# Fetched rows spread differently over the groups of the values' stage, with VectorE's loop written out

## The reference, cut to what matters

```python
def chunk(args):
    xb, ib, gb = args
    a = jnp.einsum('cd,ced->ce', xb, utab[ib]).astype(jnp.float32)
    coef = (gb * jax.nn.gelu(a, approximate=False)).astype(xb.dtype)
    return jnp.einsum('ce,ced->cd', coef, vtab[ib])
...
x = layer_norm(DN_ALPHA * x + (1.0 + g2) * f, ln2_g[l], ln2_b[l])
```

## Time and profile before

| | |
|---|---|
| median of 3 runs | 3972.95 us (3972.67 to 3986.3) |
| the profiled execution | 3967.34 us, its span 3965.5 us |
| TensorE matmuls | 3678.5 us busy, 93% of the span |
| VectorE | 2550.3 us, 64% |
| ScalarE, GpSimd | 1291.0 and 1165.5 us |
| values' stage | from about 2834 us to the end |

### The profile page before, as it was taken

One profiled execution on the slowest core, in us unless ns is written; L12 is line 12 of the kernel. 1 busy time (PEld: TensorE's weight loads), 2 busy tenths in 40 slices (PEclk: granted clock), 3 DMA queues, 4 the chain that ended last, 5 costly groups with the idle time before them and its releaser, 6 DMA issues. The chain is left out here.

```text
span 3965.5 us, 53964 instructions
## 1 busy us (share of the span) xinstructions
PE 3678.5 (93%) x19170; PEld 3215.8 (81%) x19170; DVE 2550.3 (64%) x5738; ACT 1291.0 (33%) x2513; POOL 1165.5 (29%) x797
## 2 busy tenths in 40 slices
PE   5989899998988889899998999999789999999997
PEld 3679788886766778899998999999668888888875
DVE  5663133221664521578998888988677777777777
ACT  1110122221115221222236787878512222222220
POOL 1133121211333021234443333333253333333340
PEclk9899999998998999999999999999899999999998
DMA  5841212213744222345556999999988888877782
GB/s 191 317 147 40 85 60 76 77 71 140 244 164 176 75 90 74 130 165 200 200 187 207 310 321 308 328 313 322 302 298 291 290 290 289 289 287 286 287 310 112
DMA packets 502716, 827.71 MB, mean 209 GB/s; under 512 B 289047, under 2 KB 309783, under 8 KB 496312
## 3 DMA queue, kind: packets, MB, share of 16 engines
q1 hardware_dynamic: 111848, 371.07, 26.8%
q0 software_dynamic: 84096, 318.80, 22.3%
q10 hardware_dynamic: 306576, 135.28, 13.7%
HBM read 680.35 MB, written 144.70 MB: 208 GB/s over the span
## 5 line engine op out<-in xcount | busy, mean ns | idle before, releaser
L79 PE MATMUL va_fps<-va_vt_h,va_c_h 128*128 128x512 f32 x1536 | 605.2, 394 | 62.4 <-DVE va_vt_l L2286 24.4
L80 PE MATMUL va_fps<-va_vt_l,va_c_h 128*128 128x512 f32 x1536 | 603.4, 393 | 0.0
L81 PE MATMUL va_fps<-va_vt_h,va_c_l 128*128 128x512 f32 x1536 | 602.8, 392 | 0.0
L2164 POOL DMA_INDIRECT va_rows<-in_vtab,k_pick x256 | 398.9, 1558 | 644.3 <-DVE k_big L2310 566.1
L79 PE MATMUL ga_aps<-k_u_h,k_ut_h 128*128 128x384 f32 x1152 | 399.1, 346 | 6.0 <-DVE k_ut_l L2066 4.7
L79 PEld LDWEIGHTS va_fps<-va_vt_h,va_c_h 128*128 128x128 f32 x1536 | 292.1, 190 | 127.6 <-issue 32.8
L1990 ACT ACTIVATE ga_first<-ga_first,ga_gs 128x128 f16<-128x128 f16 x1152 | 357.7, 390 | 105.6 <-DVE ga_first L2049 104.4
L81 PE MATMUL ga_aps<-k_u_h,k_ut_l 128*128 128x384 f32 x1152 | 386.9, 336 | 0.0
L80 PE MATMUL ga_aps<-k_u_l,k_ut_h 128*128 128x384 f32 x1152 | 386.4, 335 | 0.0
L2310 DVE SCALAR_TENSOR_TENSOR k_big<-va_rows,va_coef,k_big 128x1024 f32<-128x1024 f32 x254 | 320.5, 1281 | 59.7 <-DMA va_rows<-in_vtab,k_pick 59.2
L81 PEld LDWEIGHTS va_fps<-va_vt_h,va_c_l 128*128 128x128 f32 x1536 | 291.7, 190 | 61.4
(11 more groups left out here) (305 smaller groups left out, 7949.9 us busy)
## 6 DMA issues: line engine op xcount, KB each, us to landing
k_ut<-in_utab SPq DMA_DIRECT2D x129, 512.0 KB, 5.4
va_vt<-in_vtab SPq DMA_DIRECT2D x128, 512.0 KB, 6.7
va_c<-scratch_ahead SPq DMA_DIRECT2D x128, 384.0 KB, 3.3
va_wt<-scratch_gates SPq DMA_DIRECT2D x128, 384.0 KB, 5.0
hy_tab<-in_tab POOLq DMA_DIRECT2D x64, 512.0 KB, 5.4
scratch_ahead<-ga_gelu_a ACTq DMA_DIRECT2D x72, 384.0 KB, 5.8
sp_wada<-in_w_ada SPq DMA_DIRECT2D x24, 1024.0 KB, 9.1
scratch_gates<-ga_wide ACTq DMA_DIRECT2D x32, 768.0 KB, 13.2
```

Source lines behind the costliest of these rows:

```text
L79: nc.tensor.matmul(out, w[0], x[0], start=first, stop=False)
L80: nc.tensor.matmul(out, w[0], x[1], start=False, stop=False)
L81: return nc.tensor.matmul(out, w[1], x[0], start=False, stop=last)
L2164: nc.gpsimd.indirect_dma_start(got[:, q % SLOTS_G, :], None, vrows, picked(K, q)).then_inc(got_in[q % SLOTS_G], 16)
```

## The change

The number of rows taken in group 0 becomes 4, in group 1 it becomes 8, in groups 2 to 27 it becomes 9, in group 28 it becomes 6 and in group 29 it becomes 4 (again 256 in all). The five places of a group get their rows by an even cut: with nine rows 1, 2, 2, 2 and 2; with eight 1, 2, 1, 2 and 2; with six 1, 1, 1, 1 and 2; with four 0, 1, 1, 1 and 1. The loop over the 26 groups is replaced by straight code, in which the slots' numbers and the waits' values are constants. The sequences of the other four engines are not changed.

```diff
--- before.py
+++ after.py
@@ -2297,26 +2297,26 @@
                 dve.wait_ge(f_mm, j + 1)
                 v.tensor_copy(sums[:, GATHERED + STAY + j, :], wide_banks(STAY)).then_inc(f_ok, 1)
 
-            def take_row(turn, j, first=False):
-
-                k, n = j % SLOTS_G, j % GATHERED
-                i = turn + j // SLOTS_G
-                dve.wait_ge(got_in[k], 16 * (i + 1))
-                share = coef[:, n, bass.ds(SLOTS_G // GATHERED * i + k // GATHERED, 1)]
-                if first:
+            def take_row(q):
+                k, n = q % SLOTS_G, q % GATHERED
+                dve.wait_ge(got_in[k], 16 * (q // SLOTS_G + 1))
+                share = coef[:, n, q // GATHERED:q // GATHERED + 1]
+                if q < GATHERED:
                     v.tensor_scalar(sums[:, n, :], got[:, k, :], share, None, ALU.mult).then_inc(row_used, 1)
                     return
-                hold(dve, K, row_used, SLOTS_G * i + k - GATHERED + 1 + SLOTS_G)
+                hold(dve, K, row_used, q - GATHERED + 1 + SLOTS_G)
                 v.scalar_tensor_tensor(out=sums[:, n, :], in0=got[:, k, :], scalar=share, in1=sums[:, n, :],
                                        op0=ALU.mult, op1=ALU.add).then_inc(row_used, 1)
 
-            def turn(s, g, add, start, take):
-
-                cuts = (0, take // 2, take, 2 * take, 3 * take - 1, GT * take)
+            def rows_of(g):
+                return EDGE_ROWS.get(g, 9)
+
+            def turn(s, g, add):
+                start, count = sum(rows_of(b) for b in range(g)), rows_of(g)
 
                 def take_rows(place):
-                    for j in range(cuts[place], cuts[place + 1]):
-                        take_row(start, j, isinstance(start, int) and start == 0 and j < GATHERED)
+                    for j in range(count * place // (GT + 1), count * (place + 1) // (GT + 1)):
+                        take_row(start + j)
 
                 for t in range(GT):
                     coefficients(g + 1, t)
@@ -2330,9 +2330,8 @@
                 take_rows(GT)
                 add(2)
 
-            EDGE, EACH = 3, 2
-            LOOPED = BODY // 2 - 2
-            assert 4 * GT * EDGE + 2 * LOOPED * GT * EACH == GATHERED * PICKS
+            EDGE_ROWS = {0: 4, 1: 8, BODY - 2: 6, BODY - 1: 4}
+            assert sum(rows_of(g) for g in range(BODY)) == GATHERED * PICKS
 
             dve.wait_ge(gelu_ok, 1)
             ch.link(v.tensor_tensor(coef[:, :, :], coef[:, :, :], K["share"][:, :, :], ALU.mult))
@@ -2342,11 +2341,9 @@
                 value_low(0, 0, t)
             for k in range(3):
                 dve.wait_ge(K["last_gates"][k], 16)
-            turn(0, 0, first_sums, 0, EDGE)
-            turn(1, 1, lambda j: add_sums(1, j), EDGE, EDGE)
-            with dve.Fori(1, BODY // 2 - 1) as i:
-                for s in range(2):
-                    turn(s, 2 * i + s, lambda j: add_sums(2 * i + s, j), 2 * EDGE + 2 * EACH * (i - 1) + EACH * s, EACH)
+            turn(0, 0, first_sums)
+            for g in range(1, BODY - 2):
+                turn(g % 2, g, lambda j: add_sums(g, j))
             gate2 = K["ada_row"][:, 2:4, :].rearrange("p a b -> p (a b)")
 
             def residual(k):
@@ -2362,8 +2359,8 @@
                     ch.link(v.scalar_tensor_tensor(out=r, in0=x1[:, k % 2, :], scalar=ALPHA, in1=r, op0=ALU.mult, op1=ALU.add))
                 v.sem_inc(x1_used, 1)
 
-            turn(0, BODY - 2, lambda j: add_sums(BODY - 2, j), 2 * EDGE + 2 * EACH * LOOPED, EDGE)
-            turn(1, BODY - 1, lambda j: add_sums(BODY - 1, j), 3 * EDGE + 2 * EACH * LOOPED, EDGE)
+            turn(0, BODY - 2, lambda j: add_sums(BODY - 2, j))
+            turn(1, BODY - 1, lambda j: add_sums(BODY - 1, j))
             for t in range(GT):
                 coefficients(NG - 1, t)
                 residual(t)
```

## The result

The changed kernel takes 3946.57 us in the median of six runs (3938.09 to 3957.66), the one before 3975.22 in six runs of its own (3972.67 to 3986.3). The ratio is 0.9921, with a 95% interval of 0.9906 to 0.9937: some 31 us faster, and the interval leaves 25 to 37. A second set of five runs beside other kernels gave 0.9895 (0.9879 to 0.9912).

A forecast was written before the change was run, and what follows sets the result against it. TensorE bounds the kernel, with waits to win only at the ends of the values' stage. Terms 16.9 + 5.0 + 3.7 + 6.2 = 31.8 us take 3967.34 to 3935.5, or 3941 for the median; range 3932 to 3956.

The forecast's parts named there:

- The first wait: TensorE's 5.42 us wait for group 0's first copy, behind low parts needing a late value tile: stays, no gain.
- Group 0 to group 1: Waits of 5.98 and 5.95 us for the second and third copies go, with slow matmuls behind them: gain 16.9 us.
- Rival 1: First groups' loads are late where the rows were; 7 to 14 us not gained, 3948 to 3955; chance 0.13.
- Group 1: Eight rows instead of twelve: add(0) to the next takes 32.64 us instead of 37.64, gain 5.0.
- Group 28: Six rows instead of twelve: 36.35 us becomes 32.64, gain 3.7.
- The last groups: Group 29 and last loads: second coefficient starts 3.8 us after the group's end on TensorE instead of 10.0, gain 6.2.
- The inner groups: Nine rows instead of eight in 26 groups: supply suffices and TensorE hides it all, gain 0.
- The straight code: Written-out code for 26 groups: register instructions vanish, off TensorE's path, and longer code costs nothing; gain 0.
- Rival 2: Inner groups' row round trip exceeds 14.5 us; each us above costs 58 us in all, ending slower; chance 0.09.
- Rivals 3 to 5: Tail gives its part back (0.08, 3947); first wait goes as well (0.06, 3934); no change to waits (0.02, 3973).
- rival 3: Tail bound by x1's loads or the last gates, not the order: its 6.2 us given back, 3947; chance 0.08.

The follow-up runs named there:

- h_load: Changed kernel with the last two tiles' coefficients and values loaded ahead of the fourth and fifth x1 block: stage 1076.3 us, ratio 0.9893 to the kernel before.

## Why the prediction was right

The forecast was 3941 us with a range of 3932 to 3956, and the median came to 3946.57. The gain was 31.0 us of the stage where 31.8 was forecast, and it lay where the prediction had put it. That leaves 4.8 of the distance of 5.6 us; 2.3 of it is that the six runs of before have a higher median than the three that were known, and for the rest there is nothing but the chance of runs, which differ by 20 us here. The mechanism was right; that single terms came out to 0.1 us is luck, as the traces of kernels with the same first groups differ by 2.6 us there.

Term by term, with what answers to the earlier trace rows from the changed kernel, add(0) of groups 28 and 29 and the second coefficient of the last group:

```profile
3780.35 1.22 DVE L2294 TENSOR_TENSOR k_big<-k_big,va_fps 128x1024 f32<-128x1024 f32 x1 [1.54 <-PE va_fps L81]
...
3812.99 1.22 DVE L2294 TENSOR_TENSOR k_big<-k_big,va_fps 128x1024 f32<-128x1024 f32 x1 [1.55 <-PE va_fps L81]
...
3843.99 0.95 DVE L2278 TENSOR_TENSOR va_c<-va_c,va_wt 128x768 f32<-128x768 f32 x1
```

- *The first wait stays*: 5.42 before, 5.43 now. In the other six traces with these first groups it is 3.3 to 5.1.
- *Group 0 to group 1, 16.9*: add(0) of group 1 started 65.0 us after the stage's first matmul and now starts 48.0 after it (2899.07 − 2851.03): 17.0. The second copy, of which I said that it would end 1.0 us before it is needed, ended 1.0 us before (2884.1 against 2885.1). Over all traces the start takes 47.6 us in the mean of seven with four rows, 64.6 in the mean of three with twelve: 17.0 again. Rival 1 began at these copies, and did not happen: no trace with four rows and the copies' old places has a wait at the second or the third.
- *Group 1, 5.0*: 32.64 (2931.71 − 2899.07) instead of 37.64: 5.0.
- *Group 28, 3.7*: 32.64 (3812.99 − 3780.35) instead of 36.35: 3.7.
- *The last groups, 6.2*: from add(0) of group 29 to TensorE's restart 59.4 us before, 53.2 now (3866.16 − 3812.99): 6.2. Then 0.9 us was given back, which no term had. TensorE's last restart (3888.34) is followed by some three more slow matmuls than before, and the fifth of the products that go ahead of the norms, which waited 0.45 for TensorE, waits 1.09:

```profile
3917.95 1.23 DVE L2379 TENSOR_TENSOR va_mix<-va_fps,k_ada_row 128x1024 f32<-128x1024 f32 x1 [1.09 <-PE va_fps L81]
```

 That accounts for 0.6. But it need not be the change's doing: from the restart for the last low part to the end, the eleven traces with the old loads take 69.2 to 72.0 us, whatever their rows, and the one of before has the shortest. I had written that the norms set the end "as before"; they nearly do, but in this trace TensorE is about a microsecond behind what they need.
- *The inner groups, nothing*: 32.64 in all 26. VectorE idled 68 us for rows in 2952:3800, 35 before, and it cost nothing. In nearly all inner groups the eighth row came late, as the prediction has it, by 0.5 to 2.0 us; the first row of the group behind it came later still, by 1.2 to 2.6, and it had not named that one.
- *The straight code, nothing*: the run without the new order says the same, but for the 3.6 us that have no cause there. The prediction's 414 rows are a count that no view here shows; by the source 26 groups of 24 instructions on tiles stand where the loop had 46.

Rival 2, the slots' trip, was rightly small. Its mechanism exists: the limit lies between ten and eleven rows, where a trip of 12.4 us has it (32.64 × 4 / 12.4 = 10.5), and not at nine. GpSimd's issues have indeed become longer, a median of 1698 ns beside 947 in the earlier trace rows:

```profile
L2164 POOL DMA_INDIRECT va_rows<-in_vtab,k_pick x223: 942/1698/3757, 2954.4 to 3762.9; - x112
```

The longest issues, of 3.75 us, were 26 in 2952:3800 before, one to a group, and are 49 now, about two to a group (the prediction had three). All of them begin 0.3 to 0.4 us into a row behind which the two low parts follow at once, and end 0.9 us after these, about as long as the shortest issue takes (0.94): one of the changed kernel runs from 3005.81 to 3009.56, while the second low part starts at 3007.51 and the next instruction at 3008.65. The Trainium skill (SBUF — State Buffer, "SBUF: two separate sides") has the shared port pair as a lock between GpSimd and a VectorE instruction with two SBUF inputs, the latter only against a GpSimd instruction that reads SBUF. Here the fetch reads its indices (`k_pick`), and the low parts and the rows have two SBUF inputs, so these issues agree with it. The time did not feel them, since the median issue is 1.7 of a trip of 12. No run here shows which instruction held which port.

Rivals 3 to 5 did not happen in the changed kernel. The tail was in fact bound by its loads, as rival 3 has it, but in a way that the sum had already counted; h_load shows that some 8 us more lay in it.

## What to carry to other kernels

When side work is spread over the groups of a loop that another engine paces, find the groups where that engine waits, and move the side work to those where it doesn't, up to what the buffers' round trip allows: pace × slots / trip units a group. Where an addition waits behind a fetch in one engine's order, the price is not the fetch but the wait of the engine behind it, and, behind a long one, its slow clock after that. And read the stage by itself and by its parts: counted from its first matmul, two traces of one kernel agreed to 1.1 us, where whole runs of it differed by 20, but parts with the same instructions differed by up to 2.6 us between traces. Two gains that add up to the right sum may each hold some of that chance.

## What the runs showed of the hardware

Four slots of 512 KB each, refilled by indirect DMAs from GpSimd, gave one row in 3.1 us under constant load, with 309 GB/s over the core's DMA engines, all other loads included; six slots gave 348 GB/s at a DMA share of 0.92 with the same engines beside them. The lower clock follows a wait unevenly. With eleven rows, 14 waits of 0.6 to 1.95 us were followed by no slow matmul, and the same holds for one of 3.42 us in the kernel before (at 3830.99). With twelve, one of 2.09 us (at 3219.36) was followed, after four matmuls at the full clock, by eight or so 0.42 or 0.43 us apart instead of 0.23. So the length of a wait alone didn't decide it here.
